# Three square output projections by Strassen's seven products

## The reference

```python
y = jnp.concatenate([fourier_mix(u_f), o], axis=-1) @ w_out                       # layer 1, 768 tokens
o_lat = ob.transpose(1, 0, 4, 2, 3, 5).reshape(B_, S, Q_WIDTH) @ w_att_out[j]     # layer 2, 512 tokens
...
h_lat = h_lat + ga1 * o_lat
...
x = x + g1 * (jnp.concatenate([y_rw_lat, y_hg_lat], axis=-1) @ w_out[l])          # layer 3, 512 tokens
```

## Time and profile before

| what | value |
|---|---|
| median of 3 runs | 3797.2 us (3796.49 to 3800.63) |
| span of the profiled execution (the page gives no other time for it) | 3795.7 us |
| TensorE busy | 3481.4 us, 92% |
| VectorE, ScalarE, GpSimd busy | 1187.4, 820.5, 250.3 us |
| evo, first matmul to the last one's end | 374.4 to 459.6 us |
| ato | 1434.1 to 1489.1 us |
| out | 2865.9 to 2923.3 us |

### The profile page before, as it was taken

One profiled execution on the slowest core, in us unless ns is written; L12 is line 12 of the kernel. 1 busy time (PEld: TensorE's weight loads), 2 busy tenths in 40 slices (PEclk: granted clock), 3 DMA queues, 4 the chain that ended last, 5 costly groups with the idle time before them and its releaser, 6 DMA issues. The chain is left out here.

```text
span 3795.7 us, 64521 instructions
## 1 busy us (share of the span) xinstructions
PE 3481.4 (92%) x26712; PEld 2101.4 (55%) x26712; DVE 1187.4 (31%) x2684; ACT 820.5 (22%) x1495; POOL 250.3 (7%) x420
## 2 busy tenths in 40 slices
PE   6998899999998998999999869997997899999984
PEld 2557555555555584444444459994573466655543
DVE  1214122222002352222117664432332433333324
ACT  2122121111001152111103233234322122222211
POOL 0000000000000000000010000000000133333320
PEclk9999999999999999999999869998998999999996
DMA  5320123311111102452121000001102499999996
GB/s 214 124 99 29 67 101 143 133 50 34 61 46 60 43 14 78 182 195 72 69 85 52 17 2 4 4 4 53 57 18 83 155 355 353 364 354 360 349 393 226
DMA packets 104531, 484.24 MB, mean 128 GB/s; under 512 B 17682, under 2 KB 21810, under 8 KB 66560
## 3 DMA queue, kind: packets, MB, share of 16 engines
q1 hardware_dynamic: 87792, 442.88, 31.9%
q0 software_dynamic: 16528, 38.25, 3.0%
HBM read 466.11 MB, written 31.46 MB: 131 GB/s over the span
## 5 line engine op out<-in xcount | busy, mean ns | idle before, releaser
L639 PE MATMUL psum<-arena 128*128 128x512 f32 x1408 | 670.2, 596 | 10.0 <-ACT arena L401 10.0
L515 PE MATMUL psum<-arena 128*128 128x512 f32 x1088 | 515.6, 600 | 24.8 <-PEq L618 11.0
L639 PEld LDWEIGHTS psum<-arena 128*128 128x128 f32 x1408 | 264.8, 190 | 211.5 <-issue 191.2
L3045 PE MATMUL psum<-arena 128*64 128x256 f32 x3072 | 352.6, 378 | 16.2 <-DMA arena<-exp_w_in 15.1
L3045 PEld LDWEIGHTS psum<-arena 128*64 128x64 f32 x3072 | 231.8, 134 | 161.8 <-issue 54.0
L515 PEld LDWEIGHTS psum<-arena 128*128 128x128 f32 x1088 | 208.0, 192 | 188.5 <-issue 175.0
L676 DVE SCALAR_TENSOR_TENSOR arena<-psum,arena 128x511 f32<-128x511 f32 (+1 forms) x132 | 83.2, 658 | 607.1 <-ACT arena L657 607.1
L657 ACT ACTIVATE arena<-psum,arena 128x768 f32<-128x768 f32 (+1 forms) x88 | 77.9, 885 | 696.3 <-PE psum L641 416.9
L641 PEld LDWEIGHTS psum<-arena 128*128 128x128 f32 x704 | 133.7, 190 | 170.8 <-issue 170.8
L641 PE MATMUL psum<-arena 128*128 128x256 f32 x704 | 210.4, 379 | 0.0
L597 DVE SCALAR_TENSOR_TENSOR arena<-psum,arena 128x512 f32<-128x512 f32 (+1 forms) x56 | 36.3, 672 | 539.1 <-PE psum L517 293.0
(11 more groups left out here) (505 smaller groups left out, 4759.6 us busy)
## 6 DMA issues: line engine op xcount, KB each, us to landing
arena<-exp_w_in SPq DMA_DIRECT2D x207, 1024.0 KB, 10.4
arena<-w_mod_r_in SPq DMA_DIRECT2D x72, 1024.0 KB, 7.8
arena<-w_ffn_up_in SPq DMA_DIRECT2D x88, 512.0 KB, 3.5
arena<-w_ffn_down_in SPq DMA_DIRECT2D x16, 1408.0 KB, 6.0
arena<-w_in_in SPq DMA_DIRECT2D x35, 512.0 KB, 3.5
arena<-yrows SPq DMA_DIRECT2D x8, 2048.0 KB, 16.6
arena<-w_even_in_in SPq DMA_DIRECT2D x17, 512.0 KB, 3.5
arena<-w_qkv_in SPq DMA_DIRECT2D x12, 512.0 KB, 3.5
```

The costliest lines, as they stand in the source:

```text
L515: mm = pe.matmul(ps[:, 2 * b, :], lhsT, src[:, k, 0:LAT], start=(k == 0), stop=(k == kt - 1))
L639: mm = pe.matmul(ps[:, 2 * b, :], lhsT, A[:, k, 0:LAT], start=(k == 0), stop=(k == KD - 1))
L3045: mm = pe.matmul(ps[64 * c:64 * c + 64, 0, 0:256], xt[u][:, k, :], wgu[w][:, k, :, c * P:(c + 1) * P], start=(k == 0), stop=(k == KD - 1))
```

## The change

The three calls of `project` become calls of `join`, which makes two output tiles (a pair) at once by Strassen's seven products in Winograd's form. The weights of a pair are split in two halves of K by two tiles (blocks A11, A12, A21, A22 of 4 x 128 weights a partition), the source in two halves of K by two halves of the tokens (B11 to B22 of 4 x h columns; h is 384 in `evo`, 256 in the others). Each product is 4 matmuls of 128 x 128 by h, so a pair has 28 and a stage 112, where there were 64 of 512 columns and, in `evo`, 64 of 256.

The source's sums T1, T2, T3 are made once a stage by VectorE, T4 by GpSimd; the weights' sums S1, S2, S3 and A12 - S2 for each pair by GpSimd. The products share partial sums in PSUM: 1, 6, 5 and 3 accumulate in one bank, 7 and 4 in another, 2 has its own, and two pairs alternate. ScalarE copies the bank out after products 1, 6 and 7 (`c1`, `c2`, `c7`), VectorE adds products 2, 5 and 4 to the copies and gates the four quarters into `X`. Weights come a pair (1 MB) at a time into two buffers in `W` (`Pairs`), laid out by `pairs` in the host's preparation of the inputs. Numbers are summed in another order and can differ in the last bits.

```diff
-        project(nc, m, "evo", evo, m["A"], [T] * KD, residual(m, T, 0, 2), squares=T, then=up)
+        join(nc, m, "evo", evo, halves(T), T, 0, 2, parts, then=up)
...
-        project(nc, m, "ato", ato, m["A"], [LAT] * KD, residual(m, LAT, 1, 2), squares=LAT, then=up)
+        join(nc, m, "ato", ato, halves(LAT), LAT, 1, 2, parts, then=up)
...
-        project(nc, m, "out", out, m["A"], [LAT] * KD, residual(m, LAT, 2, 2), squares=LAT,
-                also=lambda sp: router_tables(sp, m, io, early))
+        join(nc, m, "out", out, halves(LAT), LAT, 2, 2, parts, also=lambda sp, s: router_tables(sp, m, io, early))
...
+class Pairs:
+    KH = KD // 2
+    RAW = (OFF["W"], OFF["W"] + KF * P)
+    SUMS = {1: OFF["W"] + KF * P + 4 * KH * P, 2: OFF["W"] + 4 * KH * P}
...
+        self.order = [(0, 1), (1, 1), (0, 2), (1, 2)] + [(p, x) for p in (0, 1) for x in (6, 7, 5, 4, 3)]
+        self.order += [(p, x) for p in range(2, self.n) for x in (1, 2, 6, 7, 5, 4, 3)]
+        self.made = {job: j + 1 for j, job in enumerate(self.order)}
...
+    def load(self, m, e, p):
+        e.dma_start(m["at"](self.RAW[p % 2], 4 * self.unit), self.w[p]).then_inc(self.sems[f"w{p % 2}"], 16)
...
+    def rest(self, m, e, s):
+        for p in range(2, self.n):
+            e.wait_ge(s["mm"], self.made[p - 2, 3])
+            self.load(m, e, p)
...
+    def sums(self, pool, m, s, p):
+        a11, a21, a22, s1, s2 = (self.piece(m, p, j) for j in (0, 2, 3, 4, 5))
+        if p:
+            pool.wait_ge(s["mm"], self.made[p - 1, 5])
+        for j in (0, 2, 3):
+            self.arrived(pool, p, j)
+        pool.tensor_tensor(s1, a21, a22, ADD).then_inc(s["ws"], 1)
+        pool.wait_ge(s["ws"], 4 * p + 1)
+        pool.tensor_tensor(s2, s1, a11, SUB).then_inc(s["ws"], 1)
+        pool.tensor_tensor(a21, a11, a21, SUB).then_inc(s["ws"], 1)
+
+    def last_sum(self, pool, m, s, p):
+        a12 = self.piece(m, p, 1)
+        pool.wait_ge(s["mm"], self.made[p, 2])
+        pool.wait_ge(s["ws"], 4 * p + 2)
+        pool.tensor_tensor(a12, a12, self.piece(m, p, 5), SUB).then_inc(s["ws"], 1)
...
+class Halves:
...
+    def sums(self, dve, s):
+        t1, t2, b22 = self.block(0, 1), self.T[2], self.block(1, 1)
+        dve.tensor_tensor(t1, t1, self.block(0, 0), SUB).then_inc(s["tb"], 1)
+        dve.wait_ge(s["tb"], 1)
+        dve.tensor_tensor(t2, b22, t1, SUB).then_inc(s["tb"], 1)
+        dve.wait_ge(s["tb"], 2)
+        dve.tensor_tensor(self.T[3], t2, self.block(0, 0), SUB).then_inc(s["tb"], 1)
...
+    def last_sum(self, pool, s):
+        pool.wait_ge(s["tb"], 2)
+        pool.tensor_tensor(self.T[4], self.block(1, 0), self.T[2], SUB).then_inc(s["t4"], 1)
...
+def pair_bank(ps, q, x, h):
+
+    return ps[:, 3 * (q % 2) + {1: 0, 6: 0, 5: 0, 3: 0, 2: 1, 7: 2, 4: 2}[x], 0:h]
+
+
+def join(nc, m, name, feed, b, n, layer, which, parts, then=None, also=None, gain=None, ctx=None):
...
+        @block.sync
+        def _(sp):
+            feed.rest(m, sp, s)
+            if also is not None:
+                also(sp, s)
+            if then is not None:
+                sp.wait_ge(s["ws"], 4 * N)
+                then.behind(m, sp, feed, s["mm"])
+
+        @block.tensor
+        def _(pe):
+            for q, x in feed.order:
+                if x == 1:
+                    feed.arrived(pe, q, 0)
+                    if q >= 2:
+                        pe.wait_ge(s["c12"], q - 1)
+                if x == 2:
+                    feed.arrived(pe, q, 1)
+                    if q >= 2:
+                        pe.wait_ge(s["c11"], q - 1)
+                if x == 6:
+                    pe.wait_ge(s["ws"], 4 * q + 2)
+                    pe.wait_ge(s["tb"], 2)
+                    pe.wait_ge(s["c1"], q + 1)
+                if x == 7:
+                    pe.wait_ge(s["ws"], 4 * q + 3)
+                    pe.wait_ge(s["tb"], 3)
+                    if q >= 2:
+                        pe.wait_ge(s["c21"], q - 1)
+                if x == 5:
+                    pe.wait_ge(s["c2"], q + 1)
+                if x == 4:
+                    pe.wait_ge(s["t4"], 1)
+                    pe.wait_ge(s["c7"], q + 1)
+                if x == 3:
+                    pe.wait_ge(s["ws"], 4 * q + 4)
+                    pe.wait_ge(s["c22"], q + 1)
+                lhsT, rhs = feed.weights(m, q, x), b.moving(x)
+                for k in range(KH):
+                    mm = pe.matmul(pair_bank(ps, q, x, h), lhsT[:, k, :], rhs[:, k, :], start=(k == 0 and x in (1, 2, 7)),
+                                   stop=(k == KH - 1), skip_group_check=x in (6, 5, 4, 3))
+                mm.then_inc(s["mm"], 1)
+
+        @block.gpsimd
+        def _(pool):
+            feed.sums(pool, m, s, 0)
+            b.last_sum(pool, s)
+            feed.last_sum(pool, m, s, 0)
+            for q in range(1, N):
+                feed.sums(pool, m, s, q)
+                feed.last_sum(pool, m, s, q)
...
+        @block.scalar
+        def _(act):
+            def square(j):
+                if j % 2:
+                    act.wait_ge(s["c12"], j // 2 + 1)
+                else:
+                    act.wait_ge(s["own"], 3 * (j // 2) + 3)
...
+            for q in range(N):
+                if q:
+                    act.wait_ge(s["own"], 3 * q - 2)
+                act.wait_ge(s["mm"], feed.made[q, 1])
+                act.activation(c1, pair_bank(ps, q, 1, h), ACT.Copy).then_inc(s["c1"], 1)
+                if q:
+                    square(2 * q - 1)
+                    act.wait_ge(s["own"], 3 * q)
+                act.wait_ge(s["mm"], feed.made[q, 6])
+                act.activation(c2, pair_bank(ps, q, 6, h), ACT.Copy).then_inc(s["c2"], 1)
+                act.wait_ge(s["mm"], feed.made[q, 7])
+                for c, (a, e, _) in zip(c7, right):
+                    out = act.activation(c, pair_bank(ps, q, 7, h)[:, a:e], ACT.Copy)
+                out.then_inc(s["c7"], 1)
+                square(2 * q)
+            square(2 * N - 1)
+
+        @block.vector
+        def _(dve):
...
+            b.sums(dve, s)
+            for q in range(N):
+                dve.wait_ge(s["c1"], q + 1)
+                dve.wait_ge(s["mm"], feed.made[q, 2])
+                dve.tensor_tensor(c1, pair_bank(ps, q, 2, h), c1, ADD).then_inc(s["c11"], 1)
+                dve.wait_ge(s["c11"], q + 1)
+                gated(2 * q, c1, h).then_inc(s["own"], 1)
+                dve.wait_ge(s["c7"], q + 1)
+                dve.wait_ge(s["mm"], feed.made[q, 5])
+                for c, (a, e, _) in zip(c7, right):
+                    out = dve.tensor_tensor(c, pair_bank(ps, q, 5, h)[:, a:e], c, ADD)
+                out.then_inc(s["c22"], 1)
+                dve.wait_ge(s["c22"], q + 1)
+                for c, (_, _, e) in zip(c7, right):
+                    out = gated(2 * q + 1, c, e)
+                out.then_inc(s["own"], 1)
+                dve.wait_ge(s["c2"], q + 1)
+                dve.wait_ge(s["mm"], feed.made[q, 4])
+                dve.tensor_tensor(c2, pair_bank(ps, q, 4, h), c2, ADD).then_inc(s["c21"], 1)
+                dve.wait_ge(s["c21"], q + 1)
+                gated(2 * q + 1, c2, h).then_inc(s["own"], 1)
+                if q:
+                    add(2 * q - 1)
+                dve.wait_ge(s["mm"], feed.made[q, 3])
+                for a, e, end in right:
+                    out = gated(2 * q, pair_bank(ps, q, 3, h)[:, a:e], end)
+                out.then_inc(s["c12"], 1)
+                if q:
+                    add(2 * q)
+            add(2 * N - 1)
```

More of the change, by code:

```diff
@@ L125, in kernel_program, with halves @@
         H = m["at"](BIG, KF, T)
+        free = BIG + 20000
+        parts = (free + 2 * T, free + 2 * T + T // 2, (free + 3 * T, free + 3 * T + P))
+        def halves(n):
+            return Halves(m, m["A"], KD // 2, n, NRM_RT, NRM_XN, free)
         evi = Feed(nc, "evi", io["w_even_in"], KD, 3)
@@ L130, in kernel_program @@
         fourier(nc, m, tables)
-        evo = Feed(nc, "evo", io["w_even_out"], KD)
+        evo = Pairs(nc, "evo", io["w_even_out"])
         gla_scan(nc, m, evo)
@@ L3242, in tiles, with pairs @@
         return v.reshape(v.shape[0] // P, P, v.shape[1] // P, P).transpose(2, 1, 0, 3).reshape(-1, P, v.shape[0])
+    def pairs(v):
+        return tiles(v).reshape(v.shape[1] // (2 * P), 2, P, v.shape[0]).transpose(0, 2, 1, 3).reshape(-1, P, 2 * v.shape[0])
     parts = {
@@ L3274 @@
         "w_in_2": tiles(x["w_in_2"][0])[[*range(4, 8), *range(4), *range(8, 15), *range(19, 27), *range(15, 19), *range(27, 35)]], "rw_w2_2": x["rw_w2_2"][0], "rw_a2_2": x["rw_a2_2"][0], "rw_g2_2": x["rw_g2_2"][0],
[L3275 removed]
+        "w_out_2": pairs(x["w_out_2"][0]), "router_w_2": x["router_w_2"][0], "router_b_2": x["router_b_2"],
         "exp_w_2": np.concatenate(
```

93 lines of the change are left out of this document (88 added, 5 removed).

## The result

The changed kernel's median is 3772.06 us over 4 runs (3768.56 to 3776.01), beside 3796.84 us for the kernel before (3795.34 to 3800.63): a ratio of 0.9934, 95% interval 0.992 to 0.9948. That is 24.8 us less, where the sum of the prediction said 21.0, and the median lies on the lower edge of the range given, 3772 to 3786. In microseconds the interval is 19.7 to 30.4, which holds the 21.0. The profiled execution took 3768.56 us, 1.9 us more than its span.

A forecast was written before the change was run, and what follows sets the result against it. TensorE was taken to bound the three stages. Columns -22.9, stall +2.8 and tails -0.9 gave -21.0 us on 3795.7, 3774.7, and with 1.5 for the median 3776.2 us; own range 3772 to 3782, 8 in 10 3772 to 3786.

The forecast's parts named there:

- Columns, -22.9: Matmuls of evo, ato and out: fewer columns save 10.3 us in evo and 6.3 each in ato and out.
- Weight loads at nothing: TensorE in the three stages: loads of about 0.19 us still hide behind records of 0.2175 us; cost zero.
- exposed-load rival: ato and out: weight loads stand exposed before 256-column records, up to +85 us, 3861 in all; chance 5%.
- Sums: VectorE's and GpSimd's two-SBUF sums queue on a shared path but stay hidden behind the products; cost zero.
- slow-sums rival: GpSimd sums of 512 take twice the estimate, about 4 us each in ato and out, 3786 in all; chance 15%.
- The stall, +2.8: Before product 6 of pair 1, waiting for ScalarE's copy: 1.1 us each in ato and out, 0.6 in evo.
- Tails, -0.9: Behind each stage's last matmul: the gated add covers half the columns, -0.9 us for three stages.
- slow-clock starts: Starts of evo and out, where TensorE's clock is below full speed: taken as unchanged, no gain or loss.
- exposed copies: Rival at 84 product boundaries: exposed copies cost 0.2 us each, +17 us, 3793 in all; chance 7%.
- late weights: Rival: pair 2 late by 1.7 us in two stages plus boundary waits, +7.6 us, 3784 in all; chance 5%.

The follow-up runs named there:

- eighth product: Changed kernel with product 3 made twice, so TensorE has as many columns as the kernel before; 3820.98 us, ratio 1.0058.
- plain order: Changed kernel with every pair's products in the order 1, 2, 6, 7, 5, 4, 3, the first two pairs as well; 3773.39 us, ratio 0.9936.
- earlier copy: Changed kernel with ScalarE copying product 1 of pair 1 ahead of the square of tile 1; 3767.63 us, ratio 0.9917.
- the weight sums: Changed kernel with GpSimd's four weight sums of a pair cut to one element, products 5 and 6 reading unsummed weights; 3788.68 us, ratio 0.9975.
- second profile: Each kernel timed and profiled again without edits: changed kernel 3771.23 us, ratio 0.9931; kernel before 3798.03 us, ratio 1.0003.
- double copies: Changed kernel with each of ScalarE's copies of products 1, 6 and 7 preceded by one into unused memory; 3776.62 us, ratio 0.9942.
- the two pauses: Changed kernel with an extra stage before the RWKV input, VectorE clearing 256 or 1400 elements of unused memory; 3776.32 and 3776.58 us, both ratios 0.9946.

## Where the prediction was right, and the step that failed

**Columns, -22.9: right.** ato without a gap is 48.69 us (48.7 predicted), 256-column records come 0.217 apart (0.2175), and the eighth product puts back 21.5 of 22.2.

**Weight loads at nothing: right.** A load of 0.19 us stands in front of each of 224 records 0.217 apart and none is seen. The exposed-load rival would have made ato and out 85 us longer. By the overlap rule of the Trainium skill (TensorE: Matmul & The Clock Gate, What overlaps and what doesn't) a weight load overlaps a running matmul only if the row groups differ; this trace disagrees, as these full 128-row loads do hide.

**Sums: right.** A GpSimd sum of 512 takes 1.27 us (1.24 estimated), T1 to T3 and S1 to S3 queue as taken from the earlier trace rows (T2 and T3 last 2.18 us each for it), and no sum releases a product in any of the three stages. The margin is thin: S3 is ready 1.9 us ahead of its use in ato, and in plain order the same sums cost ato two gaps. The slow-sums rival is out; weights were never waited for either.

**The stall, +2.8: mechanism and place right, size nearly.** One gap per stage, before product 6 of pair 1, put down to ScalarE. Its idle time, 0.76, 0.67 and 0.67, is 2.1 us; its cost is 0.9 in ato by the stretch with and without it, and with the same 0.2 on top of each idle time 2.8 in all. evo's share was taken too low (0.6), ato's and out's too high (1.1). The earlier copy removes all of it, the weight sums account for 0.27 of the 0.67.

**Tails, -0.9: a little more.** From the last matmul to the norm's first, evo went from 4.75 to 3.69 us, ato from 3.47 to 3.05, out from 3.45 to 3.48: -1.5.

**What failed** is the sentence that the slow-clock starts "stay as they are: what comes before them is untouched", and with it the tacit step that the stages without an edit keep their time. Both were put at nothing. These stages have the same instructions and another clock. What repeats in both profiles of each kernel:
- the RWKV scan: the clock returns 8.5 us behind its start instead of 15.0 or 15.1, worth 2.0 us (1.6 in the second profile).
- the norm behind ato: 1.10 us in place of 2.05 for its two records, 0.9 less. The norm behind out does the reverse, 2.04 in place of 1.10. That the two cancel in the sum is luck.

The norms behind ato and out in the kernel before (the changed kernel's are in the timeline at the top):

```profile
1492.86 2.05 PE L465 MATMUL psum<-arena 128*128 128x512 f32 x2 [3.47 <-PEq L491]
...
2927.05 1.10 PE L465 MATMUL psum<-arena 128*128 128x512 f32 x2 [3.45 <-PEq L491]
```

What does not repeat are the starts of evo and out, where the kernel before stands against itself. Its first profile lost 2.4 us at evo's start (4.8 us at 0.51) and 2.5 at out's (5.5 us at 0.55), its second 1.8 and 1.7; the changed kernel loses 1.7 and 1.8 (5.2 us at 0.68, 6.2 at 0.71). So the three stretches lost 22.0 us between the first profiles and 20.5 between the second ones, beside the 20.1 of columns and stall. Out's window in the first profile of the kernel before:

```profile
2865.90:2871.40 5.50, 5.44 (x7) 2.38 (x8) 0.00 (x0) 0.00 (x0) 0.00 (x0) 0.55 0.00 0
```

The tails' 0.6, 0.3 in front of ato (TensorE's idle time there is 1.55 us instead of 1.85) and the scan's 1.6 to 2.0 turn -21.0 into some -23.7. The comparisons gave -24.8 and -26.9; the last 1 to 3 us are well within the intervals, and whether any of them belongs to the change stays open. The other kernels bear the scan's part out: plain order, double copies and the two pauses make the same products and have the late return. With their own gaps and pauses set off they are 22.0 to 23.2 us faster than the kernel before (an interval of one such comparison is over 10 us wide, so it is the agreement of the four that counts).

That the clock's return is what lengthened or shortened the scan is read off the records; that in the scan it belongs to the program is supported by the repeats (early twice in the changed kernel and in five edits of it, late twice in the kernel before). Why the changed kernel gets the early return isn't shown. The range should have allowed for it. Its bounds, 3774.6 and 3781.6 with 2 us of scatter on each side, give 3772.6 to 3783.6, written down as 3772 to 3782; there was nothing in them for a shift of this kind, which the pauses show to be as large as 3 us in a kernel whose work is the same. The second median, 3771.23, is 0.8 us outside.

The rivals on the other side did not come near: no exposed copies (doubling them all adds 0.9 us to the gaps), no late weights.

## What to carry to other kernels

A product scheme that saves an eighth of the columns turns it into time nearly in full (21.5 of 22.2 us here) if each product is long enough to hide one copy, one sum and one weight load; look for the exception where a hand-made order brings a consumer forward and leaves its producer's queue as it was, and reorder that queue (here one copy ahead of one square: 2.8 us by the traces, 3.6 between the medians). A gap on TensorE costs more than its idle time, here about a quarter of a microsecond more each. When a change shifts a long kernel in time, allow some 4 us either way for the places where TensorE wakes from idleness, and compare marks in unchanged stages before a difference of that size is put down to the edit; when an idle stretch is bridged with extra matmuls, look at how much of it is left (with 1.0 us out started at full speed, with 3.3 it did not) and at what the next stages lose (the whole gained nothing measurable).

## What the runs showed of the hardware

- VectorE and GpSimd operations with two SBUF inputs exclude each other for a whole instruction at a time and take turns: 1.23 and 1.27 us alone, 2.18 and about 2.2 in alternation. A VectorE add with an operand in PSUM kept its 0.42 us beside a GpSimd sum.
- Behind 19 us of idle TensorE the full clock came back 8.5 us into the scan or anywhere from 13.0 to 15.1, with identical instructions. Six programs had the early return and nine a late one, and each of the two kernels that were profiled twice repeated its own.
- A matmul record of 256 f32 columns is in flight for 0.37 us and 0.217 behind the one ahead; a stall cost 0.24 us more than its idle time shows (0.91 for 0.67), two together 0.54 more (1.67 for 1.13).
